# Row strides of 1088 and 4160 bytes for split activations and split weights

## The reference

```python
h = rms_norm(x, norm_mix_g[l])
proj = h @ w_in[l] + b_in[l]                     # 1024 -> 4864
...                                              # RWKV-7, RG-LRU and gates
x = x + merged @ w_mix_out[l]
x = x + cross_attention(...)                     # w_cq, w_ckv, w_co
u = h @ w_in                                     # 1024 -> 5632
return (gelu(causal_dwconv(u[..., :D_FF])) * u[..., D_FF:]) @ w_out
```

## Time and profile before

| | |
|---|---|
| time, median of three runs | 2059.77 us (2059.16 to 2060.35) |
| profiled execution, first to last instruction (span) | 2056.6 us |
| TensorE matmuls busy | 2022.7 us, 13588 instructions |
| TensorE weight loads busy | 1805.3 us |
| VectorE busy | 1354.7 us |
| ScalarE busy | 1090.2 us |
| mean rate of the DMA engines | 175 GB/s |

### The profile page before, as it was taken

How to read it: one execution, slowest core, us unless ns; L and a number is a source line. 1 busy time by engine, 2 the same in 40 slices (tenths; PEclk the granted TensorE clock), 3 DMA queues, 4 the chain that set the end, 5 groups by cost and what they waited for, 6 DMA issues and landing times.

```text
span 2056.6 us, 34241 instructions
## 1 busy us (share of the span) xinstructions
PE 2022.7 (98%) x13588; PEld 1805.3 (88%) x13588; DVE 1354.7 (66%) x1909; ACT 1090.2 (53%) x1739; POOL 49.6 (2%) x47
## 2 busy tenths in 40 slices
PE   7999999999999999999999999999999999999998
PEld 7989988999888889899988888888899999887887
DVE  6786866777466657866766654655477667756554
ACT  5846555554454454555466444644454555645443
POOL 0021000000000000000100000000000001000000
PEclk9999999999999999999999999999999999999999
DMA  7522454565566557544553655565566535445553
GB/s 273 168 75 84 158 171 167 188 195 187 170 214 186 191 166 224 182 134 128 200 196 133 215 184 186 184 204 186 192 194 186 179 115 166 162 157 192 184 184 123
DMA packets 98716, 359.08 MB, mean 175 GB/s; under 512 B 11192, under 2 KB 11512, under 8 KB 98296
## 3 DMA queue, kind: packets, MB, share of 16 engines
q1 hardware_dynamic: 98560, 356.90, 52.8%
HBM read 353.65 MB, written 1.05 MB: 172 GB/s over the span
## 4 chain that ended last, share of the span: by engine, by line
PE 90%; DVE 6%; ACT 3%; issue 1%; DMA 0%; DVEq 0%; SPq 0%; ACTq 0%
PE ps L974 10%; PE ps L975 9%; PE ps L976 9%; PE ps L962 8%; PE ps L1148 8%; PE ps L1150 8%; PE ps L1149 8%; PE ps L1041 6%; PE ps L1039 6%; PE ps L1040 6%; DVE wlo L1640 2%; PE ps L1118 1%; PE ps L1119 1%; PE ps L1125 1%; PE ps L1006 1%; PE ps L1007 1%
## 5 line engine op out<-in xcount | busy, mean ns | idle before, releaser
L1640 DVE TENSOR_TENSOR wlo<-raw,whi 128x1024 fp32r<-128x1024 f32 x635 | 774.4, 1228 | 411.6 <-ACT whi L2372 408.2
L2372 ACT ACTIVATE whi<-raw 128x1024 fp32r<-128x1024 f32 x635 | 666.6, 1057 | 415.4 <-PE ps L1041 152.3
L974 PE MATMUL ps<-H,whi 128*128 128x256 f32 x1328 | 383.7, 289 | 1.7 <-DVE wlo L1640 1.7
L976 PE MATMUL ps<-H,wlo 128*128 128x256 f32 x1328 | 375.6, 283 | 0.0
L975 PE MATMUL ps<-L,whi 128*128 128x256 f32 x1328 | 375.5, 283 | 0.0
L1148 PE MATMUL ps<-whi,H 128*128 128x512 f32 x704 | 279.6, 397 | 3.7 <-DVE wlo L1640 1.9
L1150 PE MATMUL ps<-whi,L 128*128 128x512 f32 x704 | 275.3, 391 | 0.0
L1149 PE MATMUL ps<-wlo,H 128*128 128x512 f32 x704 | 274.8, 390 | 0.0
L974 PEld LDWEIGHTS ps<-H,whi 128*128 128x128 f32 x1328 | 254.3, 191 | 7.7 <-issue 4.4
L975 PEld LDWEIGHTS ps<-L,whi 128*128 128x128 f32 x1328 | 254.5, 192 | 0.5
L976 PEld LDWEIGHTS ps<-H,wlo 128*128 128x128 f32 x1328 | 254.3, 192 | 0.0
(11 more groups left out here) (438 smaller groups left out, 3276.2 us busy)
## 6 DMA issues: line engine op xcount, KB each, us to landing
raw<-in_ws SPq DMA_DIRECT2D x635, 512.0 KB, 3.4
prow<-in_rows SPq DMA_DIRECT2D x11, 512.0 KB, 5.9
row<-in_rows SPq DMA_DIRECT2D x9, 512.0 KB, 6.4
mema<-in_memT SPq DMA_DIRECT2D x4, 512.0 KB, 4.8
mema<-in_mem2T SPq DMA_DIRECT2D x4, 512.0 KB, 6.3
memb<-in_mem2T SPq DMA_DIRECT2D x4, 512.0 KB, 5.2
DT<-in_dec SPq DMA_DIRECT2D x2, 768.0 KB, 6.5
X<-in_x SPq DMA_DIRECT2D x1, 1024.0 KB, 10.4
```

The costliest lines, as they stand in the source:

```text
L974: e.matmul(o, h, hs[k], start=first and k == 0, stop=False, skip_group_check=True)
L976: mm = e.matmul(o, lo, hs[k], start=False, stop=last and end, skip_group_check=True)
L1640: e.tensor_tensor(m.wlo[:, n % SPL, :], r, h.bitcast(F32), SUB).then_inc(*c.lo.done(n))
L2372: e.activation(m.whi[:, n % SPL, :], m.raw[:, n % RAW, :], ACT.Copy).then_inc(*c.hi.done(n))
```

## The change

Rows of `H` and `L` become 272 numbers (1088 bytes) long, of which the first 256 are used, and slots of `whi` and `wlo` 1040 numbers (4160 bytes), of which the first 1024 are used. The start of the region behind them is rounded up to 512 bytes where it was 64. No line that issues an instruction changes; where two rows of `H` or `L` were written as one run they are now two.

```diff
+APART = 16
...
-        self.whi = kept("whi", [128, SPL, UT * 128], F32R)
-        self.wlo = kept("wlo", [128, SPL, UT * 128], F32R)
+        self.whi_slots = kept("whi", [128, SPL, UT * 128 + APART], F32R)
+        self.wlo_slots = kept("wlo", [128, SPL, UT * 128 + APART], F32R)
+        self.whi, self.wlo = self.whi_slots[:, :, 0:UT * 128], self.wlo_slots[:, :, 0:UT * 128]
         self.X = kept("X", [128, 2, 1024])
-        self.H = kept("H", [128, 8, T], F32R)
-        self.L = kept("L", [128, 8, T], F32R)
+        self.H_rows = kept("H", [128, 8, T + APART], F32R)
+        self.L_rows = kept("L", [128, 8, T + APART], F32R)
+        self.H, self.L = self.H_rows[:, :, 0:T], self.L_rows[:, :, 0:T]
...
-        low = (nc.sbuf_base + 63) // 64 * 64
+        low = (nc.sbuf_base + 511) // 512 * 512
```

## The result

The changed kernel takes 2066.02 us (median of nine runs, 2064.67 to 2068.07) against 2059.77 us for the kernel before on the same chip (2058.88 to 2060.35). The ratio is 1.0031, with a 95% interval of 1.0021 to 1.0041: slower, by 6.25 us. The profiled execution has a span of 2062.7 us, 6.1 us more than before. Lines of the file that issue instructions have numbers three higher than before: L974 is L977, L1148 is L1151, L1039 is L1042, L1640 is L1643.

The account below looks back on a forecast made before the run. TensorE was taken to bound the kernel; -10.2 us for the 256-column form and +17.0 for the 512-column form gave +6.8 us, moving the median from 2059.77 to 2066.6 us. The range was 2042 to 2083.

Parts of the forecast that it names:

- 256-column form: Matmuls in `product` and `head`, weight tile stationary, 256 activation columns moving: 6204 x 3/4 x -2.2 ns = -10.2 us.
- 512-column form: Matmuls in `wide_row`, `outward_product`, `moving`, activations stationary, 512 weights moving: 4500 at +5.5 ns for three quarters, +17.0 us net.
- What bounds: TensorE, busy 2022.7 of 2056.6 us: a nanosecond more or less between two matmuls goes straight into the end.
- Terms at nothing: Instructions, waits, DMAs, base addresses, writers and splitters: cost 0, splitting bounded at 0.3 us.
- A stall between two reads: On TensorE, both forms lose 13.3 ns per matmul; if moving read and weight load stall, relative addresses decide it.
- WH's 36 matmuls: Matmuls on operand WH, 320 bytes past a 512 multiple, started every 117.7 ns against 120.0 on H: about -2.2 ns.
- 256 acts as 0: Address distances count modulo 256 bytes, since BH at 256 kept 120.0 ns; three quarters of all pairs leave the old relation.
- Size per pair: Price per matmul at a changed distance: -2.2 ns in the 256-column form, +5.5 ns in the 512-column form.
- Settled and unsettled: A steady phase between TensorE's two reads is cheaper than unsettled in the 512-column form, dearer in the 256-column form.
- both forms gain: Rival, chance 0.28: the 512-column form saves 2.2 ns too, -17.7 us over all split matmuls, 2042.1 us.
- nothing changes: Rival, chance 0.22: the 32 cycles lost per matmul are a fixed price in both forms, 2059.8 us.
- the 512-column form pays everywhere and the other gains nothing: Rival, chance 0.10: each change of distance throws the 512-column form out of phase, +24.7 us, 2084.5 us.

Follow-up runs that it names:

- the first program: Not a kernel variant: series of both matmul forms alone, moving tensor at thirteen starting addresses, weights aligned; 113.3 ns at 192 bytes in the 256-column form, 226.7 at 256 in the 512-column form.
- the second program: Not a kernel variant: series of both forms at 23 distances behind three disturbances, four with weights shifted too; both operands at 64 bytes gave 120.0 and 226.7 ns.

## Why the prediction was right

**The sum.** Forecast +6.8 us, measured +6.25. Its two terms were -10.2 us for the 256-column form and +17.0 for the 512-column form; the trace shows -10.8 and +16.9. That is as near as it is by some luck: the means without waits moved by -2.0 and +4.1 ns, which over 6204 and 4500 matmuls would be -12.4 and +18.5 us, and the intervals around waits and breaks took some of both back.

**What bounds.** That nanoseconds between matmuls go straight into the end held. The intervals of TensorE always add up to the span; what shows it is that nothing else on it moved, 242.7 against 242.8 us, and the intervals with waits by +2.1 and -2.4 us.

**Terms at nothing.** The splitters keep 1227 and 1057 ns in the rows of after, and the writers of H and L theirs (L<-ps,H takes 684 ns at the mean there too). Slots 4352 bytes apart, which move all that lies behind them, take 2059.68 against 2059.78 us.

**A stall between two reads.** Right in that addresses decide, and now shown by experiment and not only by WH's 36 matmuls: the pace depends on the distance between the moving and the stationary operand, and both moved together change nothing. That the two reads stall each other is the reading that fits; which of the two loads, the matmul's own or the next one's, is not shown. The part "256 acts as 0" is right too.

**Size per pair.** Here errors offset each other, and the nearness of the sum is luck. I let a quarter of the pairs keep their pace and gave every other distance the same value, -2.2 ns, the row of WH, or +5.5. In the series 64, 128 and 192 bytes are worth -2.2, -1.4 and -6.7 ns in the 256-column form, a mean of -2.6 over the four residues, where I had -1.65; the kernel shows -2.0. In the 512-column form they cost 2.2, 6.6 and 6.6, a mean of 3.9, where I had 4.1; the kernel shows 4.1. But the kernel does not get there by these steps: its quarter at distance 0 moved by -1.5 and +2.5 ns, about -2 and +3 us, where I had nothing, and its quarter at 192 bytes gained 2.4 ns of the 6.7. The 5.5 ns were taken from nine unsettled intervals and lie amid those prices.

**Settled and unsettled.** This picture was half right. The new paces are not only the old ones thrown out of phase: with a constant distance they are steady themselves, and some distances have more than one. But in the changed kernel the distance seldom stays long enough for them. What most of its matmuls show is a pace soon after a change, near 118 and 230 to 233 ns at every distance, and near it lie also the unsettled paces of the earlier trace rows on which the forecast rested. How much of the 6.25 us is the price of the distances and how much that of changing between them, no run separates.

**The rivals.** That both forms gain is refuted by every distance tried: the lowest pace of the 512-column form was 226.7. That nothing changes is refuted as well. The Trainium skill, page "SBUF — State Buffer", section "Who interferes with whom", calls the two read ports of TensorE independent. The series of the first program differ by up to 6.7 ns with nothing but a distance between the two reads changed, so here the measurement decides against independence in time. That the 512-column form pays everywhere and the other gains nothing is refuted by the 256-column rows and by the 2084 us it asked for, but its mechanism, that each change of distance throws the phase out, has a part: it is why distance 0 costs 229.8 ns in the changed kernel. The five intervals that I held against it were of the 256-column form alone.

## What to carry to other kernels

Where TensorE is the bound and each matmul brings its own weights, look at the distance from start to start, not at the durations, and compare it with the columns' own time. Then treat the address of the moving operand less that of the stationary one, modulo 256 bytes, as a parameter. For the slots a pad of 256 bytes was free; another pad moved a 256-column matmul by up to 7 ns down and a 512-column matmul by up to 7 up, at 240 bytes by 10. A distance that changes from matmul to matmul gives neither the best pace nor the old one. The sign counts, and an operand that is moving in one form and stationary in another wants a different place in each. Measure in the kernel itself: 112 bytes was among the best distances in a series and brought the kernel 3 us of the 40 expected.

## What the runs showed of the hardware

The pace of split matmuls at 2.4 GHz depends on the distance between two reads of TensorE itself: 113.3 to 120.0 ns for 256 columns and 226.7 to 233.3 for 512 in the series of the first program, which is 6.7 to 13.3 ns over the columns' own 106.7 in the one and 13.3 to 20.0 over 213.3 in the other. In the second program a 512-column series at 240 bytes took 236.7. Behind a change of distance or a break some nine intervals pass before such a pace is steady. The best distance for one form, 192 bytes, is among the worst for the other.

At one distance there can be two steady phases, 113.3 and 117.8 ns, kept for long stretches. The times of such a kernel also spread more, 2042.82 to 2051.43 us for the one with the constant 64 bytes, against 2058.28 to 2060.14 for the kernel before beside it. That the phases are why fits, but is not shown, since one execution of each was profiled. What picks the phase stays open; the second program shows that the matmuls just ahead have a part in it.

Why 64 and 192 bytes differ, and where the period of 256 bytes comes from, was not settled: no run here tells the memory from the engine that reads it.
